# The sample's differential keys and values: fetched page by page by SyncE through a register, in place of GpSimd's row gathers

## The chip, the cores and the metric

One program on one core of a Trainium2 chip computes a whole decoder layer. The metric is the device time of the program in microseconds, the median of several executions. The core has five engines that run their own instruction streams and meet only at semaphores: TensorE (PE, its weight loads are shown as PEld), VectorE (DVE), ScalarE (ACT), GpSimd (POOL) and SyncE (SP). All of them can issue transfers, which run on the core's 16 DMA engines.

## The reference, cut to what matters

The layer runs for a prompt of 1024 tokens and for a sample group of 8 sequences with 4 new tokens each. Each sample sequence has 4096 past tokens in a paged cache. A page holds 128 tokens, and `page_table` (8 x 32, int32) says which page of the pool holds which part of a sequence. The part that the change touches is the sample's differential attention:

```
def gather_pages(pool, page_table):
    rows = pool[page_table]
    return rows.reshape((page_table.shape[0], -1) + pool.shape[2:])
...
def diff_sample(qb, kb, vb, cache_k, cache_v, page_table, bias_b, lam, lam_init, subln_g):
    t = qb.shape[1]
    past = page_table.shape[1] * cache_k.shape[1]
    k_all = jnp.concatenate([gather_pages(cache_k, page_table).astype(kb.dtype), kb], axis=1)
    v_all = jnp.concatenate([gather_pages(cache_v, page_table).astype(vb.dtype), vb], axis=1)
    return diff_core(qb, k_all, v_all, past + jnp.arange(t), jnp.arange(past + t), bias_b, lam, lam_init, subln_g)
```

All of `cache_b_k` and `cache_b_v` that the table names is read: 8 sequences x 32 pages x 128 tokens x 512 float32, for keys and again for values, 134 MB in all. The same sample group also has a selective attention ("A", smaller caches `cache_a_k`, `cache_a_v`) and an indexer (`cache_idx_k`), which the change leaves with GpSimd.

## The kernel before

The program is a row of stages. The one that matters is `selective_and_sample_stage`. In it two streams of steps are interleaved into one fixed order (function `beside`), the same on PE, ACT and DVE: the prompt's selective attention (lines 1374 to 1500) and the sample's attention (class `Walk` and `sample_attention`). GpSimd and SyncE have their own programs in the stage, `pool` and `sync`.

The sample's attention first scores the indexer's keys (steps "i"), then walks over chunks of past tokens. There are 32 differential ("B") chunks, 16 for each of two groups g of four sequences, then the selective ("A") ones. A B chunk is 256 tokens, that is two pages, of four sequences j = 0 to 3. Its data are a **unit** u: four tiles of keys and four of values, each 128 partitions x 1024 float32 (512 KB), 4.19 MB together. Partition p of a tile holds two neighbouring tokens (`RKB` is 2), so a page of 128 tokens fills 64 partitions, and the chunk's first page lies in partitions 0 to 63, the second in 64 to 127.

On PE, a chunk n goes through these steps: "k" transposes the keys of each j through PSUM (line 1875, two banks of four transposes each; ACT copies each bank out, line 2004), "s" makes the logits (line 1895), DVE takes their maximum (line 2130), ACT the exponential (line 2014), "p" transposes the probabilities (line 1937), and "o" multiplies them with the values (line 1958). The keys of chunk n + 1 are turned before the outputs of chunk n. Steps "c" (lines 1852 and 2058) are a search for the indexer's threshold, and lines 1412 to 1438 belong to the prompt's stream; both fill the time between.

Keys have one buffer for each j (`kv[:, j, :]`, in the tile `region`), so the keys of unit u + 1 may be fetched once PE has turned those of u (semaphore `t_full`). Values have two: `kv[:, 4 + j, :]` for even units, and for odd ones `apart` (tiles `sa_more_values` and `side`); those of unit u may be fetched once unit u - 2 has been used (`pv_done`). GpSimd fetches both: `gather_rows` (line 1109) is one indirect DMA of 128 rows of 4 KB, whose row numbers stand in a column of the table `gather_b`, computed once by DVE. It issues the four keys of a unit as their buffers come free, and then the four values. SyncE has little to do in the stage: one load at its start, half of `w_out` when the mask is ready (line 1788), and the other half after the last output.

Of the kernel before, what the change touches and what calls it, by code (L numbers as in the profile page):

```python
# [22 lines left out]
P = 128  # L23
# [190 lines left out]
class Setup:  # L214
# [57 lines left out]
    def other_loads(self, sp):  # L272
        M, io = self.M, self.io

        def load(dst, src):
            sp.dma_start(dst, src).then_inc(self.loaded, 16)
            self.n_loaded += 16
        load(M.const[:], io["consts"][:, 0:M.const.shape[1]])
        load(M.const_setup, io["consts"][:, M.const.shape[1]:])
        load(self.rb32, io["rel_bias"][:])  # L280
        for t in range(4):
            load(self.rb4[32 * t:32 * t + 32, :], io["rel_bias"][:])
        load(M.gain_ak[:], io["a_k_norm"][0].partition_broadcast(P))
# [71 lines left out]
    def dve(self, eng, s, room):  # L355
# [38 lines left out]
        if 2 <= s < 5:  # L394
            n, rk, table = (("b", RKB, M.gather_b), ("a", RKA, M.gather_a), ("i", RKI, M.gather_i))[s - 2]
# [1162 lines left out]
class Walk:  # L1558
# [73 lines left out]
    def keys_arrivals(self, u, j):  # L1632

        if u < self.first_a:
            return NCI + u + 1
        i = self.turn(u, j)
        return (NCI + self.first_a if i % 6 < 4 else self.first_a // 2) + i // 6 + 1

    def values_arrivals(self, u, j):

        if u < self.first_a:
            return (u + 1) // 2 if self.aside(u) else NCI + u // 2 + 1
        i = self.turn(u, j)
        return (NCI if i % 6 < 4 else 0) + self.first_a // 2 + i // 6 + 1
# [14 lines left out]
def sample_attention(nc, io, M, K, S):  # L1659
# [7 lines left out]
    kv_rows = {("B", 0): io["cache_b_k"][0].rearrange("n (s r) h c d -> (n s) (r h c d)", r=RKB),  # L1667
               ("B", 1): io["cache_b_v"][0].rearrange("n (s r) h d -> (n s) (r h d)", r=RKB),
               ("A", 0): io["cache_a_k"][0].rearrange("n (s r) g d -> (n s) (r g d)", r=RKA),
# [26 lines left out]

    def keys_at(u, j):

        x = walk.turn(u, j) % 6 if u >= walk.first_a else j
        return (kv[:, x, :], loaded[x]) if x < 4 else (apart[x - 4], M.gathered_apart[x - 4])  # L1700

    def values_at(u, j):

        if walk.aside(u):
            return apart[j], M.gathered_apart[j]
# [9 lines left out]
    def pool(eng):  # L1715
# [17 lines left out]
        def keys(u, js=range(4)):  # L1733
            for j in js:
                i = walk.turn(u, j)
                if u == 0:
                    eng.wait_ge(t_full, fill["i", NCI - 1, 0, 1, j] + 1)
                elif i < 4:
# [7 lines left out]
        def values(u):  # L1746
            for j in range(4):
                i = walk.turn(u, j)
                if u == 0:
                    eng.wait_ge(t_full, fill["i", NCI - 1, 1, 1, j] + 1)  # L1750
                elif u == 1 and j == 0:
                    eng.wait_ge(sc_mm, NCI)
                elif 0 <= i - 4 < 2:
# [11 lines left out]
        keys(0)  # L1765
        values(0)
        for u in range(1, len(walk.units)):
# [1516 lines left out]
def build(nc, io, const_at):  # L3284
    with ExitStack() as ctx:
# [7 lines left out]
        M.x_loaded = [ctx.enter_context(nc.semaphore(f"x_loaded{t}")) for t in range(NT)]  # L3293
        M.gathered_apart = [ctx.enter_context(nc.semaphore(f"gathered_apart{i}")) for i in range(4)]
# [34 lines left out]
        with ExitStack() as c1:  # L3329
# [10 lines left out]
            with ExitStack() as c2:  # L3340
                M.bias_s = sb(c2, "bias_s", [P, 2, P])
                M.bias_new = sb(c2, "bias_new", [P, 2, 2, NS])
                M.gather_b = sb(c2, "gather_b", [P, DEC_B * NCB], I32)
# [134 lines left out]
```

## Time and profile before

| | |
|---|---|
| median of 3 runs | 2584.93 us (2583.08 to 2594.52) |
| the profiled execution | span 2590.7 us |
| PE busy | 2312.3 us, 89% of the span |
| DVE, ACT, POOL busy | 1103.6, 766.2 and 660.5 us (43%, 30%, 25%) |
| moved by GpSimd's queue (q0) | 48384 packets, 176.18 MB |
| moved by SyncE's queue (q1) | 80774 packets, 90.50 MB |

The span runs from the first to the last instruction of one execution, taken by the profiler; that execution lies 5.8 us above the median. Busy time is summed over the whole program, though the stages have different limits, so the stage that the change touches (about 565 us to 1330 us) has to be read by itself. Issuing a DMA does not count as busy time on SP; an indirect DMA on POOL does.

### The profile page before, as it was taken

The numbers are of one execution on the slowest core, as the hardware profiler recorded it, in microseconds if no ns is written. First come the engines' busy times: TensorE is split into PE (matmuls) and PEld (weight loads), VectorE is DVE, ScalarE is ACT, GpSimd is POOL, SyncE is SP. The second block draws the span as 40 slices with busy tenths as digits, with TensorE's granted clock in tenths as the row PEclk, the third lists the DMA queues.
The fourth block names the chain that finished last, engine by engine and source line by source line (L and its number), as shares of the span: only waits on it lengthen the run. The fifth ranks groups of instructions, "written<-read, shape, count | busy, mean of one in ns | idle before, by whom it ended". The sixth has DMA issues, their size and how long they took to land. (4 is left out here: it accounts for less than half of the span.)

```text
span 2590.7 us, 32530 instructions
## 1 busy us (share of the span) xinstructions
PE 2312.3 (89%) x12169; PEld 1549.6 (60%) x12189; DVE 1103.6 (43%) x2687; ACT 766.2 (30%) x2065; POOL 660.5 (25%) x703
## 2 busy tenths in 40 slices
PE   7999997767777878788789898899999999999999
PEld 5644443443455455555444445548888888888887
DVE  5489998742445533333322212352443343371001
ACT  3551345653444444444421013311111111110000
POOL 1451223123544445433301010013222121201110
PEclk9999998988889889998889999999999999999999
DMA  4211101025888778765540014111111111122221
GB/s 140 73 60 70 38 9 65 1 82 188 275 277 269 234 266 281 257 213 193 173 162 28 33 49 163 34 67 34 50 34 50 34 50 40 44 65 74 74 63 39
DMA packets 147603, 281.75 MB, mean 109 GB/s; under 512 B 13479, under 2 KB 82775, under 8 KB 147447
## 3 DMA queue, kind: packets, MB, share of 16 engines
q0 software_dynamic: 48384, 176.18, 20.2%
q1 hardware_dynamic: 80774, 90.50, 10.6%
q10 hardware_dynamic: 18288, 12.98, 1.7%
q8 instruction: 99, 1.62, 0.2%
q14 instruction: 58, 0.47, 0.1%
HBM read 261.68 MB, written 17.94 MB: 108 GB/s over the span
## 5 line engine op out<-in xcount | busy, mean ns | idle before, releaser
L634 PE MATMUL PS<-region 128*128 128x512 f32 (+5 forms) x864 | 327.7, 534 | 1.8 <-DMA region<-w_in 1.8
L2784 PE MATMUL PS<-region,ffn_w 128*128 128x264 f32 x1408 | 323.1, 388 | 1.6 <-PEq L2234 1.6
L2784 PEld LDWEIGHTS PS<-region,ffn_w 128*128 128x128 f32 x1408 | 269.2, 191 | 48.4 <-issue 1.9
L2004 ACT COPY region<-PS 128x512 f32<-128x512 f32 x352 | 197.2, 591 | 212.6 <-PE PS L1868 72.2
L634 PEld LDWEIGHTS PS<-region 128*128 128x128 f32 (+1 forms) x864 | 152.7, 181 | 161.2 <-issue 140.9
L2784 PE MATMUL PS<-region,side 128*128 128x264 f32 x1056 | 245.0, 389 | 1.8 <-POOL side L2741 1.8
L1875 PE MATMUL PS<-ident_f,region 128*128 128x128 f32 x1024 | 170.7, 316 | 82.4 <-ACT region L2004 44.1
L2784 PEld LDWEIGHTS PS<-region,side 128*128 128x128 f32 x1056 | 200.0, 191 | 35.8 <-POOL side L2741 1.9
L1875 PEld LDWEIGHTS PS<-ident_f,region 128*128 128x128 f32 x1024 | 133.5, 162 | 117.0 <-issue 76.3
L931 DVE TENSOR_SCALAR_CACHE_REDUCE mask<-score,cand 128x384 bf16<-128x384 f32 (+2 forms) x198 | 180.9, 942 | 3.4
L1109 POOL DMA_INDIRECT region<-cache_b_k,gather_b x128 | 120.4, 941 | 212.0 <-PE PS L1875 177.8
L2739 POOL TENSOR_TENSOR side<-ffn_w 128x512 f32<-128x512 f32 x22 | 28.4, 1290 | 393.2 <-DMA ffn_w<-w_gate 199.6
L2931 DVE TENSOR_TENSOR ffn_gb<-PS,ffn_u 128x264 f32<-128x264 f32 (+2 forms) x66 | 20.5, 338 | 183.2 <-ACT ffn_u L2895 120.7
L2304 PE MATMUL PS<-side,QTB 128*128 128x512 f32 x192 | 85.4, 594 | 0.9 <-PEq L2660 0.9
L2374 DVE TENSOR_TENSOR region<-PS,region 128x512 f32<-128x512 f32 (+1 forms) x36 | 24.8, 688 | 136.3 <-PE PS L2304 136.3
L2150 DVE SCALAR_TENSOR_TENSOR sa_oacc<-sa_oacc,sa_alpha,PS 128x512 f32<-128x512 f32 (+1 forms) x48 | 29.5, 614 | 100.2 <-PE PS L1958 82.3
L1109 POOL DMA_INDIRECT region<-cache_b_v,gather_b x64 | 60.2, 940 | 42.1 <-PE PS L1958 20.7
L3120 PE MATMUL PS<-H,ffn_w 128*128 128x264 f32 x308 | 69.8, 386 | 1.3 <-PEq L2728 1.3
L2130 DVE TENSOR_REDUCE sa_cmax<-PS 128x1 f32<-128x256 f32 (+2 forms) x48 | 23.1, 482 | 110.6 <-remote 86.2
L2864 ACT COPY side<-PS 128x264 f32<-128x264 f32 x44 | 16.7, 379 | 180.6 <-PE PS L2784 180.6
L1478 DVE TENSOR_REDUCE sa_a_far_max<-PS 128x1 f32<-128x16 f32 (+6 forms) x56 | 31.8, 569 | 88.7 <-PE PS L1419 71.1
L3258 DVE TENSOR_TENSOR dn_rest<-PS,dn_rest 128x512 f32<-128x512 f32 (+2 forms) x24 | 11.6, 510 | 135.4 <-PE PS L3131 134.9
(448 smaller groups left out, 4017.7 us busy)
## 6 DMA issues: line engine op xcount, KB each, us to landing
ffn_w<-w_gate SPq DMA_DIRECT2D x11, 1024.0 KB, 5.4
ffn_w<-w_up SPq DMA_DIRECT2D x11, 1024.0 KB, 5.5
region<-w_in SPq DMA_DIRECT2D x4, 2048.0 KB, 7.9
ffn_w<-w_down ACTq DMA_DIRECT2D x7, 704.0 KB, 5.6
region<-x_prompt ACTq DMA_DIRECT2D x8, 512.0 KB, 7.1
region<-x_prompt SPq DMA_DIRECT2D x8, 512.0 KB, 10.6
mem_keys<-cache_mem_k SPq DMA_DIRECT2D x8, 512.0 KB, 5.0
mem_values<-cache_mem_v SPq DMA_DIRECT2D x8, 512.0 KB, 8.0
```

What stands on the lines that cost most here:

```text
L634: last = nc.tensor.matmul(M.PS[0:n, s % 3, 0:chunks[j].width], XT[:, c, t * P:t * P + n], w[j % 2][:, c, 0:chunks[j].width], start=(c == 0 ...
L931: self.link.send(nc.vector.tensor_scalar(self.mask[:, sc], self.score[:, sc], as_float[:, x:x + 1], 0.0, op, ALU.add, accum_out=self.count ...
L1109: nc.gpsimd.indirect_dma_start(out, None, src, bass.IndirectOffsetOnAxis(ap=table[:, col:col + 1], axis=0)).then_inc(arrived, 16)
L1478: nc.vector.tensor_reduce(far_max[:, e:e + 1], slot(e, 0, lo), axis=AX.X, op=ALU.max).then_inc(far_done, 1)
L1875: last = nc.tensor.transpose(t[:, q * P:(q + 1) * P], keys[:, r * 512 + m * P:r * 512 + (m + 1) * P], K("ident"))
L2004: nc.scalar.copy(dst, M.PS[0:dst.shape[0], T0 + x % 2, 0:dst.shape[1]]).then_inc(t_read, 1)
L2150: nc.vector.scalar_tensor_tensor(oacc[:, 0:kw], oacc[:, 0:kw], alpha[:, x], M.PS[:, L1, 0:kw], ALU.mult, ALU.add).then_inc(o_done, 1)
L2304: last = nc.tensor.matmul(M.PS[:, s % 4, :], lhs(c, t), w[q][:, c, :], start=(c == 0), stop=(c == kc - 1))
L2374: nc.vector.tensor_tensor(x, M.PS[0:n, s % 4, :], x, ALU.add).then_inc(added, 1)
L2739: nc.gpsimd.tensor_tensor(ws[:, 0], a21, a22, ALU.add).then_inc(made, 1)
L2784: last = nc.tensor.matmul(M.PS[:, bank, 0:TW], left[:, c, :], right[:, c, :], start=begin and c == 0, stop=(c == KH - 1), skip_group_check ...
L3120: last = nc.tensor.matmul(M.PS[:, bank + x, 0:TW], left[:, c, :], right[:, c, x * TW:(x + 1) * TW], start=begin and c == 0, stop=(c == KH ...
```

## The change

SyncE takes over the 256 fetches of the B units. It loads the page table itself into an 8 x 32 tile, `pages`. For each unit, each j and each of its two pages it reads the page number into a register (`value_load`), and issues a plain DMA from that page into the 64 partitions that belong to it. The eight registers read for a unit's keys are used again for its values. So a tile comes in two DMAs of 256 KB where it came in one gather of 512 KB: 512 DMAs and 256 register loads in place of 256 gathers. The waits are the same ones, in the same order, now on SyncE. The B tiles get semaphores of their own, since the counts of the gathers' semaphores now hold only indexer and A fetches; the table `gather_b` and the four DVE instructions that made it go.

```diff
@@ other_loads
+        sp.dma_start(M.pages[:], io["page_table"][:]).then_inc(M.pages_loaded, 16)
...
@@ pool
-            if kind == "B":
-                gather(out, arrived, kv_rows[kind, v], M.gather_b, (4 * g + j) * NCB + c)
-            else:
-                gather(out, arrived, kv_rows[kind, v], M.gather_a, (4 * g + j) * NCA + c // HALVES)
+            gather(out, arrived, kv_rows[kind, v], M.gather_a, (4 * g + j) * NCA + c // HALVES)
...
-        keys(0)
-        values(0)
-        for u in range(1, len(walk.units)):
+        for u in range(walk.first_a, len(walk.units)):
...
@@ sync
+        half, n_pool = P // 2, io["cache_b_k"].shape[1]
+        eng.wait_ge(M.pages_loaded, 16)
+        for u in range(walk.first_a):
+            kind, g, c = chunks[walk.units[u]]
+            page = {}
+            for v in range(2):
+                for j in range(4):
+                    b = 4 * g + j
+                    if v == 0 and u == 0:
+                        eng.wait_ge(t_full, fill["i", NCI - 1, 0, 1, j] + 1)
+                    elif v == 0:
+                        eng.wait_ge(t_full, fill["k", walk.units[u - 1], j, 1] + 1)
+                    elif u == 0:
+                        eng.wait_ge(t_full, fill["i", NCI - 1, 1, 1, j] + 1)
+                    elif u == 1 and j == 0:
+                        eng.wait_ge(sc_mm, NCI)
+                    elif j == 0:
+                        eng.wait_ge(pv_done, walk.units[u - 2] + 1)
+                    out, arrived = (values_at if v else keys_at)(u, j)
+                    for i in range(2):
+                        if v == 0:
+                            page[j, i] = eng.value_load(M.pages[b:b + 1, 2 * c + i:2 * c + i + 1], min_val=0,
+                                                        max_val=n_pool - 1)
+                        eng.dma_start(out[half * i:half * (i + 1), :],
+                                      pages_b[v][bass.ds(page[j, i], 1)].rearrange("o s f -> (o s) f")
+                                      ).then_inc(arrived, 16)
         for x in range(2):
             if x == 0:
                 eng.wait_ge(mask_ready, 1)
```

GpSimd's program in the stage before, from the indexer's gathers to the B values of unit 3 (`gather_i`, `gather_b` are the tables of row numbers; brackets name the semaphores waited for):

```order
L1109 DMA region<-cache_idx_k,gather_i 128x1024 [waits sa_t_full] x4
L1109 DMA region<-cache_b_k,gather_b 128x1024 [waits sa_t_full] x4
L1109 DMA region<-cache_b_v,gather_b 128x1024 [waits sa_t_full] x4
L1109 DMA region<-cache_b_k,gather_b 128x1024 [waits sa_t_full] x4
L1109 DMA sa_more_values<-cache_b_v,gather_b 128x1024 [waits sa_sc_mm]
L1109 DMA sa_more_values<-cache_b_v,gather_b 128x1024
L1109 DMA side<-cache_b_v,gather_b 128x1024 x2
L1109 DMA region<-cache_b_k,gather_b 128x1024 [waits sa_t_full] x4
L1109 DMA region<-cache_b_v,gather_b 128x1024 [waits sa_pv_done]
L1109 DMA region<-cache_b_v,gather_b 128x1024 x3
```

The same place of GpSimd's program after the change:

```order
L1110 DMA region<-cache_idx_k,gather_i 128x1024 [waits sa_t_full] x4
L1110 DMA region<-cache_a_k,gather_a 128x1024 [waits sa_t_full] x4
L1110 DMA region<-cache_a_v,gather_a 128x1024 [waits sa_pv_done]
L1110 DMA region<-cache_a_v,gather_a 128x1024 x3
L1110 DMA sa_more_values<-cache_a_k,gather_a 128x1024 [waits sa_pv_done] x2
```

All 256 B gathers are gone from GpSimd, and the A gathers follow the indexer's at once. SyncE's program in the stage before, whole (it ends with the first loads of the next stage):

```order
L1536 UNCONDITIONAL_BRANCH [waits barrier_Pool_Activation_PE_DVE_SP_release]
L1399 DMA bias_a<-bias_scratch 128x8x256
L1788 DMA side<-w_out 128x4x512 [waits sa_mask_ready]
L1788 DMA side<-w_out 128x4x512 [waits sa_pv_done]
L1535 UNCONDITIONAL_BRANCH
```

SyncE's program after it, from the last two keys of unit 0 to the first key of unit 1 (`TENSOR_LOAD` is the register load; each `ISA` row is a register operation or check that belongs to it or to the DMA's address):

```order
L1799 TENSOR_LOAD pages [waits sa_t_full]
L1799 ISA x2
L1801 ISA
L1801 DMA region<-cache_b_k 64x1024
L1799 TENSOR_LOAD pages
L1799 ISA x2
L1801 ISA
L1801 DMA region<-cache_b_k 64x1024
L1801 DMA region<-cache_b_v 64x1024 [waits sa_t_full]
L1801 DMA region<-cache_b_v 64x1024
L1801 DMA region<-cache_b_v 64x1024 [waits sa_t_full]
```

Each key half is four rows, of which the first, the register load, stands behind the wait; each value half is one. The two `w_out` loads now stand behind all of them.

## Rows read from the trace of the kernel before

**Rows 1.** The page: span, DMA share and rate in 40 slices of 64.8 us.

```profile
span 2590.7 us, 32530 instructions
DMA  4211101025888778765540014111111111122221
GB/s 140 73 60 70 38 9 65 1 82 188 275 277 269 234 266 281 257 213 193 173 162 28 33 49 163 34 67 34 50 34 50 34 50 40 44 65 74 74 63 39
```

**Rows 2.** Windows: the stretch from unit 1's first key to unit 31's, and two pieces.

```profile
core 0: us, PE busy (x) PEld busy (x) DVE busy (x) ACT busy (x) POOL busy (x), PEclk, DMA share, GB/s
650.00:700.00 50.00, 37.45 (x298) 24.21 (x298) 21.25 (x76) 20.90 (x62) 24.30 (x26) 0.86 0.83 277
...
1050.00:1100.00 50.00, 38.84 (x356) 25.70 (x350) 15.93 (x44) 21.31 (x50) 24.36 (x27) 0.93 0.80 265
626.00:1102.00 476.00, 374.99 (x3200) 242.98 (x3212) 197.08 (x600) 210.02 (x538) 227.80 (x240) 0.90 0.80 266
```

**Rows 3.** Timeline of POOL: first key gathers of units 1 and 31, and unit 6.

```profile
626.49 0.94 POOL L1109 DMA_INDIRECT region<-cache_b_k,gather_b  x1 [13.92 <-PE PS L1875]
...
700.85 0.94 POOL L1109 DMA_INDIRECT region<-cache_b_k,gather_b  x1 [2.75 <-PE PS L1875]
...
706.40 0.94 POOL L1109 DMA_INDIRECT region<-cache_b_k,gather_b  x1 [0.95 <-PE PS L1875]
708.28 0.94 POOL L1109 DMA_INDIRECT region<-cache_b_v,gather_b  x1 [0.94 <-PE PS L1958]
...
712.01 0.94 POOL L1109 DMA_INDIRECT region<-cache_b_v,gather_b  x1 [0.30 <-issue]
...
715.46 0.94 POOL L1109 DMA_INDIRECT region<-cache_b_k,gather_b  x1 [2.51 <-PE PS L1875]
...
1102.28 0.93 POOL L1109 DMA_INDIRECT region<-cache_b_k,gather_b  x1 [1.36 <-remote]
```

**Rows 4.** Timeline of all engines, 707 to 716 us: one unit's logits and what follows.

```profile
708.22 1.93 PE L1895 MATMUL PS<-region,QBB 128*32 128x256 f32 x32
711.17 0.63 PE L1875 MATMUL PS<-ident_f,region 128*128 128x128 f32 x4
714.00 0.42 DVE L2130 TENSOR_REDUCE sa_cmax<-PS 128x1 f32<-128x256 f32 x1 [3.13 <-remote]
714.04 0.37 ACT L1447 COPY region<-PS 128x256 f32<-128x256 f32 x1 [5.56 <-remote]
714.53 0.66 PE L1875 MATMUL PS<-ident_f,region 128*128 128x128 f32 x4 [2.73 <-ACT sa_total L2004]
```

**Rows 5.** Waits: us in total, times, longest; then SyncE's own.

```profile
DVE sa_cmax L2130 <- remote: 80.4, 25, 5.3
...
SPq L1788 <- PE PS L1958: 430.2, 1, 430.2
SPq L1788 <- DVE sa_mask L2071: 332.4, 1, 332.4
```

**Rows 6.** Page, DMA issues: KB each, median us to landing. Stores of full and of 32 partitions.

```profile
x_scratch<-region SPq DMA_DIRECT2D x8, 512.0 KB, 2.6
p_b_v<-in_nat SPq DMA_DIRECT2D x8, 256.0 KB, 2.0
p_idx_k<-in_nat SPq DMA_DIRECT2D x8, 32.0 KB, 1.4
x_scratch<-region SPq DMA_DIRECT2D x1, 128.0 KB, 1.9
s_b_k<-in_kd SPq DMA_DIRECT2D x1, 64.0 KB, 1.6
s_idx_k<-in_nat SPq DMA_DIRECT2D x1, 8.0 KB, 1.4
```

**Rows 7.** DMA view of 1338 to 1365 us, 40 slices: SyncE's loads of 128 partitions.

```profile
GB/s 12 0 115 231 346 413 401 325 407 394 397 361 407 410 416 437 416 407 437 419 407 437 419 401 437 407 328 194 285 373 413 407 407 413 407 443 422 407 376 61
```

**Rows 8.** Timeline of SP: issues of plain loads, one behind the other.

```profile
1340.62 3.58 SPq L202 DMA_DIRECT2D region<-x_prompt  x6
...
1582.46 1.93 SPq L2550 DMA_DIRECT2D mem_keys<-cache_mem_k  x4
```

More of the change, by code:

```diff
@@ L393, in dve @@
             link(nc.vector.tensor_scalar(M.gain_sub[:], M.gain_sub[:], 1.0 - LAM0, None, ALU.mult))
-        if 2 <= s < 5:
-            n, rk, table = (("b", RKB, M.gather_b), ("a", RKA, M.gather_a), ("i", RKI, M.gather_i))[s - 2]
+        if 3 <= s < 5:
+            n, rk, table = (("a", RKA, M.gather_a), ("i", RKI, M.gather_i))[s - 3]
             pages = self.pt_f.rearrange("p (u i) -> p u i", i=rk)
@@ L1634, in keys_arrivals @@
         if u < self.first_a:
-            return NCI + u + 1
+            return 2 * (u + 1)
         i = self.turn(u, j)
-        return (NCI + self.first_a if i % 6 < 4 else self.first_a // 2) + i // 6 + 1
+        return (NCI if i % 6 < 4 else 0) + i // 6 + 1
     def values_arrivals(self, u, j):
         if u < self.first_a:
-            return (u + 1) // 2 if self.aside(u) else NCI + u // 2 + 1
+            return 2 * (u // 2 + 1)
         i = self.turn(u, j)
-        return (NCI if i % 6 < 4 else 0) + self.first_a // 2 + i // 6 + 1
+        return (NCI if i % 6 < 4 else 0) + i // 6 + 1
     def rescaled(self, n):
@@ L1666, in sample_attention @@
     idx_rows = index_rows(io)
-    kv_rows = {("B", 0): io["cache_b_k"][0].rearrange("n (s r) h c d -> (n s) (r h c d)", r=RKB),
-               ("B", 1): io["cache_b_v"][0].rearrange("n (s r) h d -> (n s) (r h d)", r=RKB),
-               ("A", 0): io["cache_a_k"][0].rearrange("n (s r) g d -> (n s) (r g d)", r=RKA),
+    pages_b = (io["cache_b_k"][0].rearrange("n (s r) h c d -> n s (r h c d)", r=RKB),
+               io["cache_b_v"][0].rearrange("n (s r) h d -> n s (r h d)", r=RKB))
+    kv_rows = {("A", 0): io["cache_a_k"][0].rearrange("n (s r) g d -> (n s) (r g d)", r=RKA),
                ("A", 1): io["cache_a_v"][0].rearrange("n (s r) g d -> (n s) (r g d)", r=RKA)}
@@ L1695, in sample_attention @@
     loaded = M.gathered
+    keys_loaded, values_loaded, apart_loaded = ([S.sem(f"{n}_loaded{j}") for j in range(4)]
+                                                for n in ("keys", "values", "apart"))
     def keys_at(u, j):
+        if u < walk.first_a:
+            return kv[:, j, :], keys_loaded[j]
         x = walk.turn(u, j) % 6 if u >= walk.first_a else j
@@ L1702, in values_at @@
     def values_at(u, j):
-        if walk.aside(u):
-            return apart[j], M.gathered_apart[j]
+        if u < walk.first_a:
+            return (apart[j], apart_loaded[j]) if walk.aside(u) else (kv[:, 4 + j, :], values_loaded[j])
         x = walk.turn(u, j) % 6 if u >= walk.first_a else j
@@ L1735, in keys @@
                 i = walk.turn(u, j)
-                if u == 0:
-                    eng.wait_ge(t_full, fill["i", NCI - 1, 0, 1, j] + 1)
-                elif i < 4:
+                if i < 4:
                     turned(u - 1, j)
@@ L1748, in values @@
                 i = walk.turn(u, j)
[L1749 to L1753, printed above, removed]
+                if 0 <= i - 4 < 2:
                     used(walk.first_a - 1)
@@ L3293, in build @@
         M.x_loaded = [ctx.enter_context(nc.semaphore(f"x_loaded{t}")) for t in range(NT)]
+        M.pages_loaded = ctx.enter_context(nc.semaphore("pages_loaded"))
         M.gathered_apart = [ctx.enter_context(nc.semaphore(f"gathered_apart{i}")) for i in range(4)]
@@ L3342, in build @@
                 M.bias_new = sb(c2, "bias_new", [P, 2, 2, NS])
-                M.gather_b = sb(c2, "gather_b", [P, DEC_B * NCB], I32)
+                M.pages = sb(c2, "pages", [DEC_B, PAST // PAGE], I32)
                 M.gather_a = sb(c2, "gather_a", [P, DEC_B * NCA], I32)
```

## The prediction

> **What bounds the kernel now.** I began with the page's slices: over the whole span the DMA engines are little used, but from 650 us on there is a plateau, shares of 7 to 8 tenths and 234 to 281 GB/s, which lasts until about 1100 us [rows 1]. That is the walk over the B units, the only place that the change touches. The timeline of POOL gives its pace: unit 1's first key gather starts at 626.49 us and unit 31's at 1102.28 [rows 3]. So 30 units take 476 us, 15.9 us each. In that stretch PE is busy 375.0 of 476 us (79%, 12.5 us for each unit), POOL 227.8, DVE 197.1, ACT 210.0; the DMA engines are at 0.80 with 266 GB/s [rows 2]. 266 GB/s x 15.9 us is 4.2 MB, one unit. So no engine is full; PE and the DMA engines are nearest, both at 80%, and 3.4 us of each unit are lost on PE.
>
> Where they are lost shows in one unit. PE issues its logits at 708.22 for 1.93 us, four key transposes at 711.17, and then nothing until 714.53 [rows 4]. DVE, which waits for those logits, starts at 714.00, and ACT, which waits for a transpose of the prompt's stream, at 714.04, both with a releaser that the profile can't name ("remote"). So what PE had finished by 710.2 reached the others 3.8 us later, all at once. In the same time POOL issues its four value gathers, the last at 712.01 for 0.94 [rows 3], and the release comes 1.05 us after its end. The waits of DVE for the logits with this unnamed releaser sum to 80.4 us in 25 times [rows 5], which is 3.2 us each and most of PE's loss. I read it as a side effect of back-to-back gathers on GpSimd, though one trace doesn't prove it. Whatever its cause, it is what this change could give back.
>
> **The change, part by part.**
>
> *POOL* loses 256 gathers of 0.94 us. They are not its bound (227.8 of 476 us), so nothing comes from its time as such. If the late releases of PE come from the gathers, up to 3.2 us for each unit is free: 30 x 3.2 = 96 us.
>
> *SyncE's issues.* SyncE waits idle for 332.4 and 430.2 us in this stage [rows 5], so its time is free, but its pace counts. It must issue 16 DMAs and 8 register loads in each unit. A plain load is issued in 0.48 us (1.93 for 4) to 0.60 us (3.58 for 6) [rows 8]; I take 0.48, since these are smaller, and 16 make 7.7 us. A register load is nowhere in the trace. From below it costs nothing; from above I take the smallest transfer's whole way, 1.4 us from issue to landing of 8 KB [rows 6], since a load of one word can hardly take longer, with its register operations. So SyncE needs 7.7 to 7.7 + 8 x 1.4 = 18.9 us for each unit. I keep both ends. As to the waits: the register load stands behind the wait for `t_full`, and what is queued behind it on SyncE is the rest of the unit and, at the very end, half of `w_out`, which is needed only in the next stage: it was issued at once when the mask was ready and will now go out some 300 us later, still before the A chunks end. A key's way gets longer by a register load, but a key buffer is refilled most of a period before PE wants it (released and gathered at 700.85, next turned at 711.17), so up to some us more are hidden.
>
> The Trainium skill gives a floor for such a load (DMA: Bandwidth & Descriptors, section "Latency and other measured facts"): about 600 ns. With it SyncE would need 12.5 us for a unit, and would bound nothing.
>
> *The transfers.* This is the term on which the sign rests. The bytes are the same, but each DMA now covers 64 partitions, and 16 engines serve it. Loads of 128 partitions on SyncE's queue run at a plateau of 407 GB/s, the value that comes most often in [rows 7]. Stores show what a narrow tile does. With all 128 partitions 32, 256 and 512 KB land after 1.4, 2.0 and 2.6 us [rows 6]: 1.37 us fixed, and 480 KB more in 1.2 us, about 410 GB/s. A tile of 32 partitions with 128 KB takes 1.9 us. On the full tiles' line it would be 1.37 + 0.32 = 1.69; it takes 0.53 us behind the fixed part, that is 247 GB/s (64 KB in 1.6 agree with 285). With landings rounded to 0.1 us, the 128 KB allow 207 to 291. So a tile in a part of the partitions moves at half to seven tenths of the full rate.
>
> A unit at 247 GB/s takes 4.19 / 0.247 = 17.0 us, at half of the loads' plateau (204 GB/s) 20.6 us, and at the full 407 only 10.3. I take 20.6. Half is what would come out if the write side of half the partitions has half the width, and the DMAs alternate between the halves in one queue, so that all 16 engines are in the same half at the same time. The store rows are single transfers whose fixed part hides some of their slowness, so I lean to the low rate.
>
> What SBUF — State Buffer in the Trainium skill says of this (section "Door 1: The DMA port swizzle") speaks against the change outright: partitions 0 to 63 reach only 8 of the 16 ports, measured there at 196 GB/s for 1 MiB against 328 for all 128. Its next section but one ("Can I just issue two DMAs to hit both halves?") adds that two concurrent DMAs on the two halves gain only 6% over one. At 196 GB/s a unit would take 21.4 us and the sum below would be 2751. The store rows agree in direction, and with a smaller loss.
>
> *Start and small things.* Unit 0 is fetched in the pause before 626 us, which has 14 us to spare [rows 3]. The four DVE instructions and the page table's load lie in the first stage beside other work. The A units are gathered as before.
>
> **Sum.** The walk becomes bound by the transfers: 30 x 20.6 = 618 us for 476, so +142. SyncE (at most 18.9 us) and PE (12.5 us) fit below that. What the gathers' end gives back to PE vanishes in the new wait, for keys and values in flight. The prompt's steps are spread through the same walk and wait with it. 2590.7 + 142 = 2733 for the profiled execution; the median lies 5.8 us below it, which gives **2727 us**.
>
> **The rivals.**
>
> 1. *The halves run together and PE is the bound (faster).* If the 16 engines drift apart, some in the lower half and some in the upper, or a narrow load is simply as fast as a wide one, transfers need 10.3 us. If then a register load costs less than (12.5 - 7.7) / 8 = 0.6 us, PE's 12.5 us rule: 30 x (12.5 - 15.9) = -101 us, 2484. For it: the late releases of PE would be gone with the gathers. Against it: the store rows, and two unknowns have to come out well at once. It turns slower where a unit needs more than 15.9 us, that is below 264 GB/s or above 1.0 us for a register load.
> 2. *Full rate, but SyncE paces.* With 1.0 us for a register load nothing changes; at 1.4 us a unit takes 18.9, +91 us, 2676.
> 3. *Narrow rate as in the stores, 17.0 us:* +33, 2618.
> 4. *SyncE is slower than I bound it.* With 2.0 us for a load and its register operations it needs 23.7 us: +235, 2820. Then keys would be what PE waits for, and SyncE would never be idle.
>
> **How the numbers follow.** Chances: the forecast 0.52, rival 1 0.20, rival 2 0.10 (half of it within 0.5% of no change), rival 3 0.08, rival 4 0.10. So faster 0.20, same 0.05, slower 0.75; 0.5% is 13 us and about what a measurement of this kernel can tell from no change. The forecast's own range is 2680 to 2770: 19.0 us for a unit, and 22.0 where waits couple with a full queue. For 8 in 10 the range has to reach to both sides: up to rival 4, 2830, and down to 2500, where rival 1 has come out all but wholly; what is left out is rival 1's best case and a worse rival 4.
>
> **What would show it.** In the profile after, the first and the last B key load should lie about 618 us apart, the windows between at some 205 GB/s with a high DMA share, as packets of 4 KB take twice as long. PE's busy time in that stretch stays at 375 us but falls to 60% of it, and its waits stand before the key transposes or the outputs. DVE's unnamed waits for the logits should be gone or rare if the gathers cause them; if they stay, that reading was wrong. SyncE should show issues of about 0.5 us and pauses in front of `t_full`; if it has none, rival 4 or 2 holds. The forecast is wrong if the rate in that stretch is above 264 GB/s.

## The result, and the profile after

The changed kernel takes 2616.1 us (median of 4, 2603.1 to 2624.2), the kernel before on the same chip 2587.4 (4 runs): a ratio of 1.011, 95% interval 1.0076 to 1.0145. It is slower, by 29 us (1.1%) and not by the 140 forecast; the range held the time. The profiled execution has a span of 2614.4 us, 23.7 more than before.

The page of the kernel after, the same lines as in [rows 1]:

```profile
span 2614.4 us, 34354 instructions
PEclk9999997988778888989879999999999999999999
DMA  3211101026999899995532023211111111122221
GB/s 138 73 59 70 38 9 65 1 86 177 243 251 251 238 230 248 279 273 192 179 124 104 2 79 123 71 67 34 33 50 49 34 50 34 49 65 69 74 63 42
```

The plateau of the B walk is still there, but most of its DMA shares are 9 tenths where they were 7 and 8, and it moves a little less: full engines, fewer bytes. The windows over the walk, to be laid beside [rows 2] (the third is again unit 1's first key to unit 31's):

```profile
650.00:700.00 50.00, 36.96 (x260) 24.90 (x264) 17.73 (x61) 20.08 (x54) 0.00 (x0) 0.76 1.04 242
1050.00:1100.00 50.00, 43.23 (x370) 28.34 (x370) 16.37 (x45) 23.39 (x56) 0.00 (x0) 0.90 1.03 283
627.66:1132.42 504.76, 396.79 (x3215) 257.79 (x3215) 196.72 (x600) 215.13 (x544) 0.00 (x0) 0.85 1.01 248
```

POOL is empty, the DMA share is 1.01 and the rate 248 GB/s. A unit takes 504.76 / 30 = 16.8 us in place of 15.9. That is +29 us. What comes before unit 1 takes 1 us more than before and what follows unit 31's first key 6 us less (2614.4 - 1132.4 against 2590.7 - 1102.3), so the walk is the whole difference. SyncE's timeline, which takes the place of POOL's in [rows 3]:

```profile
627.66 9.57 SPq L1801 DMA_DIRECT2D region<-cache_b_k  x8
637.33 2.45 SPq L1801 DMA_DIRECT2D sa_more_values<-cache_b_v  x4
639.88 2.46 SPq L1801 DMA_DIRECT2D side<-cache_b_v  x4
...
1132.42 9.54 SPq L1801 DMA_DIRECT2D region<-cache_b_k  x8
```

Eight keys with their register loads take 9.6 us, eight values 4.9: 14.5 us of a 16.8 us unit. The timeline of all engines around one unit's logits, which answers to [rows 4], and the page's DMA issues (KB each, median us from issue to landing):

```profile
716.62 1.93 PE L1916 MATMUL PS<-region,QBB 128*32 128x256 f32 x32
...
718.96 0.37 ACT L1448 COPY region<-PS 128x256 f32<-128x256 f32 x1 [2.07 <-PE PS L1428]
...
719.15 0.42 DVE L2151 TENSOR_REDUCE sa_cmax<-PS 128x1 f32<-128x256 f32 x1
```

```profile
region<-cache_b_k SPq DMA_DIRECT2D x256, 256.0 KB, 11.0
region<-cache_b_v SPq DMA_DIRECT2D x128, 256.0 KB, 10.8
```

The logits end at 718.55 and DVE reads them at 719.15, with no wait of its own in between; before it waited 3.13 us, with no releaser named. But a 256 KB key now needs 11 us to land, since it stands in a full queue. The waits of 600 to 1148 us (us in total, times, longest):

```profile
PEld PS L1896 <- DMA region<-cache_b_k: 100.1, 58, 5.1
PE PS L1896 <- DMA region<-cache_b_k: 80.0, 45, 4.8
DVE sa_cmax L2151 <- PE PS L1916: 17.9, 14, 2.7
...
SPq L1799 <- PE PS L1896: 51.0, 40, 11.1
```

DVE's 80.4 us of unnamed waits for the logits [rows 5] are gone. In their place TensorE waits 80.0 us for keys in flight.

### The profile page after: what moved, and what is told of

Its sections match the earlier page's. It is cut to its first block and busy times, and to the rows that moved or that the text cites. A ratio compares the mean times of both kernels' runs of the same rounds, so it can differ in the third digit from the quotient of the medians.

```text
span 2614.4 us, 34354 instructions
## 1 busy us (share of the span) xinstructions
PE 2335.7 (89%) x12189; PEld 1564.2 (60%) x12189; DVE 1102.1 (42%) x2683; ACT 769.3 (29%) x2065; POOL 418.1 (16%) x447
## 5 line engine op out<-in xcount | busy, mean ns | idle before, releaser
L1896 PE MATMUL PS<-ident_f,region 128*128 128x128 f32 x1024 | 180.2, 331 | 93.2 <-DMA region<-cache_b_k 80.0
L1896 PEld LDWEIGHTS PS<-ident_f,region 128*128 128x128 f32 x1024 | 144.3, 171 | 127.7 <-DMA region<-cache_b_k 100.1
L1110 POOL DMA_INDIRECT region<-cache_a_k,gather_a x22 | 21.4, 972 | 583.7 <-PE PS L1896 558.9
L1240 ACT ACTIVATE region<-PS,pb_negmax 128x384 f32<-128x384 f32 (+5 forms) x96 | 54.6, 578 | 49.8 <-DVE pb_negmax L1334 33.3
L1188 PE MATMUL PS<-KTB,QTB 64*128 64x384 f32 (+5 forms) x192 | 50.8, 621 | 20.1 <-ACT region L1240 16.6
```

The costliest lines, as they stand in the source:

```text
L1188: last = nc.tensor.matmul(out[:, k], M.QTB[s, h, i * P:(i + 1) * P], M.KTB[s, h, a:b], start=True, stop=True)
L1240: nc.scalar.activation(prob[:, 2 * (n % 2) + k, a:b], slot(piece0[n] + x, b - a)[:, k], ACT.Exp, bias=negmax[:, n % 2, k:k + 1], accum_out ...
L1896: last = nc.tensor.transpose(t[:, q * P:(q + 1) * P], keys[:, r * 512 + m * P:r * 512 + (m + 1) * P], K("ident"))
```

## The experiments

Each was timed against the kernel before on the same chip, but they ran on different chips (e1 to e4 on one; e5 to e8, e9 to e12, e13 to e15 each on one of their own; the changed kernel apart from them). A difference of two medians from different chips is therefore given by the ratios too, as a share of 2587 us. Ratios have their 95% interval. "Fixed pages" marks kernels whose B tiles come from page numbers set at build time in place of the page table's. A unit's time is from the first and the last unit on SyncE's timeline.

| kernel | median us | ratio to before |
|---|---|---|
| changed kernel | 2616.1 | 1.011 (1.0076 to 1.0145) |
| e1 halves, fixed pages | 2593.7 | 1.0026 (0.9992 to 1.0060) |
| e2 128 partitions, fixed pages | 2482.5 | 0.9599 (0.9572 to 0.9626) |
| e3 page over 128 partitions | 2513.1 | 0.9710 (0.9683 to 0.9738) |
| e4 values grouped by half | 2644.3 | 1.0229 (1.0196 to 1.0261) |
| e5 e2 + 4 small gathers a unit | 2584.4 | 0.9946 (0.9925 to 0.9966) |
| e6 e3 with fixed pages | 2487.7 | 0.9579 (0.9556 to 0.9601) |
| e7 e3, register loads first | 2516.8 | 0.9694 (0.9675 to 0.9713) |
| e8 changed kernel, loads first | 2614.2 | 1.0065 (1.0040 to 1.0090) |
| e9 e5 with 16 rows | 2586.1 | 0.9995 (0.9982 to 1.0008) |
| e10 e5 with one gather | 2488.0 | 0.9616 (0.9600 to 0.9632) |
| e11 e2 + GpSimd arithmetic | 2483.1 | 0.9601 (0.9585 to 0.9617) |
| e12 e3, values by GpSimd | 2490.9 | 0.9628 (0.9612 to 0.9645) |
| e13 lower halves only | 2493.9 | 0.9665 (0.9649 to 0.9681) |
| e14 e1, halves paired | 2633.3 | 1.0215 (1.0185 to 1.0246) |
| e15 a queue for each half | 2536.9 | 0.9836 (0.9817 to 0.9856) |

### Is it the width of the transfer? (e1, e2)

e1 takes away the register loads and keeps the two DMAs of 64 partitions:

```diff
-                        if v == 0:
-                            page[j, i] = eng.value_load(...)
+                        at = (b * NCB * 2 + 2 * c + i) % n_pool
                         eng.dma_start(out[half * i:half * (i + 1), :],
-                                      pages_b[v][bass.ds(page[j, i], 1)]...
+                                      pages_b[v][at:at + 1]...
```

> The changed kernel with fixed page numbers: the same 512 DMAs of 64 partitions on SyncE, but no register load (each B tile gets pages by count, not by the page table). Theory W (a tile in 64 partitions is written at a reduced rate, 249 GB/s in the walk after the change): nothing moves, since only SyncE's pace changes; 2616 us within 10, 16.8 us for a unit, 4 KB packets at 0.27 us. Rival I (SyncE's issuing paces the walk: 9.2 us for eight keys and 5.0 for eight values, 14.3 of 16.8 us): without the loads SyncE needs 16 x 0.62 = 9.9 us for a unit, and the walk falls towards PE's 12.5 to 14 us, 2490 to 2535 us.

e2 takes two neighbouring pages in one DMA of 128 partitions:

```diff
+                    at = (b * NCB * 2 + 2 * c) % n_pool
+                    eng.dma_start(out, pages_b[v][at:at + 2]...).then_inc(arrived, 16)
```

> As e1_half_static, but the two pages of a tile are neighbours in the pool and come in one DMA of 128 partitions x 4 KB (256 DMAs of 512 KB; page numbers fixed, not by the page table). Theory W: packets fall back to 0.16 us, the transfers need 10.3 us for a unit, and PE's 12.5 to 13.5 us become the bound: 2485 to 2520 us, below the kernel before, because GpSimd's gathers and the late releases beside them are gone too. A rival by which HBM or SyncE's queue as such is slow at these loads: the same as e1_half_static, at or above 2600 us. If the late releases had nothing to do with the gathers, they are seen again and the time is 2570 to 2590, that of the kernel before.

e1 came out at 2593.7, e2 at 2482.5: the same bytes, packets of the same 4 KB, 111 us apart. The windows 650 to 700 us, of e1 and then of e2 (columns as in [rows 2]):

```profile
650.00:700.00 50.00, 34.67 (x282) 22.08 (x282) 19.27 (x64) 19.22 (x55) 0.00 (x0) 0.88 1.04 239
```

```profile
650.00:700.00 50.00, 44.66 (x436) 27.80 (x424) 32.15 (x110) 28.31 (x83) 0.00 (x0) 1.00 1.00 380
```

Both have full DMA engines here; the wide tiles move 380 GB/s, the narrow ones 239, and PE issues 436 matmuls in place of 282. In e2 a unit takes 12.6 us (622.5 to 1001.8 us for 30), in e1 15.9 in a profiled execution that lies 12 us below its median. The 12.6 look like PE's 12.5 us of before, but are made up otherwise: PE is busy for 339.25 us of e2's walk, 11.3 a unit, and idle for 1.3. So the narrow tile is what bounds the changed kernel. e2 came out just under what theory W gave it; e1 missed both of its expectations, 22 us below theory W's 2616 and far above rival I, so what the register loads cost is not nothing. e1 against the changed kernel prices them at about 22 us, at the medians and by the ratios, but e1's runs lie wide, from 2570 to 2619 (without the two longest its median is 2590.7), and the two intervals of the ratio all but touch. e1 also reads other pages of the pool, which no run here keeps apart from the loads, and the DMA share is full with them and without (1.01 and 1.03 over the walk), so how they cost time is open.

### How fast is a half? (e4, e13, e14, e15)

e4 issues a unit's values as four lower halves and then four upper ones:

```diff
+            for i in range(2):
+                for j in range(4):
+                    out, arrived = values_at(u, j)
+                    eng.dma_start(out[half * i:half * (i + 1), :], pages_b[1][bass.ds(page[j, i], 1)]...
```

> The changed kernel, but the eight value DMAs of a unit go out as four to partitions 0 to 63 and then four to 64 to 127, in place of alternating; the rest is the same. If the 249 GB/s (above half of the full plateau of 407) come from engines that have drifted into different halves, the values now move at 204 GB/s: 2.1 MB take 10.3 in place of 8.4 us, +1.9 us for a unit, +57 us, 2665 to 2680 us. If the rate of a half doesn't depend on what the others do: 2616 us within 10.

It took 28 us more than the changed kernel (31 by the ratios), about half of the 57 that drifted engines were to cost and clearly more than the rival's nothing. e14 changes only the order in e1, so that neighbours in the queue share a half:

```diff
-                    for i in range(2):
+                    for i in ((0, 1), (1, 0))[j % 2]:
```

> The kernel with fixed page numbers and 64-partition DMAs (2594 at the median), with the halves of every second tile issued in the other order: lower, upper, upper, lower, so that two neighbours in the queue are in one half. Theory M: the queue's engines work a DMA or two apart, and it is this spread over the halves that lifts the rate above half. Then it falls a little, as with the grouped values: 2600 to 2640. Rival: the order of the halves doesn't matter: 2570 to 2619, as without.

It took 2633.3, 40 us more than e1 (49 by the ratios), with the same instructions and bytes. The walks of the two, unit 1's first key to unit 31's, e1 and then e14, both at a full DMA share:

```profile
623.60:1100.97 477.37, 378.58 (x3219) 243.84 (x3219) 196.11 (x601) 213.78 (x545) 0.00 (x0) 0.90 1.03 261
625.11:1134.28 509.17, 383.39 (x3093) 249.44 (x3093) 191.52 (x585) 207.60 (x524) 0.00 (x0) 0.85 1.03 236
```

e13 fetches, from unit 2 on, the lower halves alone, and leaves old data in the upper ones:

```diff
-                    for i in range(2):
+                    for i in range(2 if u < 2 else 1):
```

> The kernel with fixed page numbers and 64-partition DMAs, but from unit 2 on only the lower half of each tile is fetched (the upper half keeps old data), so half the bytes. Theory H: one half alone moves at half the full rate. Packets of 4 KB then take 0.32 us (twice 0.159), the rate while they move is 204 GB/s, a unit needs 2.1 MB / 204 = 10.3 us, and TensorE's 12.5 us bind: 2482 to 2500. Rival: a half alone is already as fast as the mixture of the changed kernel: packets of 0.26 us, the same time.

Its time, 2493.9, says only that TensorE is the bound again. What it was made for is the rate. The DMA view of 650 to 700 us, 40 slices of 1.25 us, first of e13, then of e2, then of the changed kernel:

```profile
DMA  9999999999999999899999957599988846389999
GB/s 206 206 210 203 203 200 206 206 213 200 197 206 206 210 210 203 161 243 200 206 210 203 206 121 200 108 288 206 197 190 213 128 154 203 66 256 206 210 210 200
```

```profile
GB/s 413 393 413 419 416 413 413 413 413 406 410 406 410 413 410 410 403 383 364 390 387 416 367 374 397 341 282 295 311 262 324 351 406 383 413 380 377 292 334 383
```

```profile
GB/s 239 239 249 226 252 256 226 252 236 239 256 239 239 252 226 243 243 243 246 256 229 252 252 229 249 246 229 249 236 246 246 249 233 233 239 249 226 256 236 239
```

One half alone moves 206 GB/s with all engines full, half of the 413 of the wide tiles. Halves that alternate in one queue move 226 to 256 in this window, 242 on the mean; paired (e14) the same window has 221, at a full share too. So a half is at half the rate, as forecast, and what the forecast missed is that alternating halves do better. That the order alone moves the rate is measured; that the engines are then in different halves at one time is the reading of it, since no view shows which half an engine is writing. e15 mixes them on purpose, lower halves by SyncE and upper by GpSimd, both with the page number in a register:

```diff
+        # GpSimd: the same loop, with i = 1
-                    for i in range(2):
+                    for i in (0,):
```

> The changed kernel with all lower halves by SyncE and all upper halves by GpSimd (plain DMAs with the page number in a register of GpSimd, which in the kernel with values by GpSimd delayed nobody). Theory M: with a queue for each half both halves are in flight together all the time, the rate goes up to 330 to 400 GB/s, and TensorE's 12.6 us bind: 2485 to 2510. Rival: the engines take the two queues in turn and a packet into half the partitions stays slow: 2580 to 2620.

2536.9 us, 79 less than the changed kernel (71 by the ratios) and between the two expectations. Its window:

```profile
650.00:700.00 50.00, 40.92 (x337) 26.73 (x339) 20.92 (x72) 25.64 (x71) 13.93 (x27) 0.89 1.03 294
```

294 GB/s at a full share, and 291 over its walk (626.68 to 1053.31 us): the mixture is better, but not full. SBUF — State Buffer in the Trainium skill (section "Can I just issue two DMAs to hit both halves?") says that two concurrent DMAs on the two halves gain 6% over one. Here 294 against e13's 206 is 43% more, and even one queue of alternating halves gains 17% (242 in the window of the changed kernel); the measurement decides. The same page's figure for one half, 196 GB/s for 1 MiB (section "Door 1: The DMA port swizzle"), is near the 206.

### SyncE's pace (e3, e6, e7, e8)

e3 keeps the page table, the register loads and 16 DMAs a unit, but spreads each page of 128 tokens over 128 partitions, 2 KB each. The order of the tokens within a tile changes, so one bias moves with it:

```diff
-                      out[half * i:half * (i + 1), :]
+                      out[:, 512 * i:512 * (i + 1)]
...
-                    for r in range(RKB):
-                        ... M.PS[:, L0, r * P + 64:(r + 1) * P], K("ident"), M.bias_s[:, 1, r:P:RKB]
+                        ... M.PS[:, L0, P:2 * P], K("ident"), M.bias_s[:, 1, 0:P]
```

> The changed kernel with another layout of the B tiles: a page's 128 tokens lie in 128 partitions, 2 KB each, the second page in the second half of the columns; register loads, number and size of the DMAs as in the changed kernel, and the whole computation is done. Theory W: width is restored, packets of 2 KB take 0.08 to 0.09 us, and SyncE's 14.3 us for a unit become the bound: 14.4 to 15.5 us, 2545 to 2580 us, faster than before. Rival I: SyncE's work is unchanged, so 2600 to 2616 us stay. A third outcome, that many small packets cost as much as narrow tiles: 2616 or more.

2513.1 us: 103 less than the changed kernel with the same work for SyncE, and 2.9% less than before. That is 32 us below the best that was expected, since SyncE, with a less full queue, needs 12.3 us for a unit in place of 14.5 (rows below). A unit takes 13.7 us, 1.1 above e2's. e6 takes the loads out of e3:

> The kernel with a page over 128 partitions, its page numbers fixed (the B pages are not those of the page table) and no register loads; still two DMAs of 2 KB a partition for each tile. Theory S: at 13.7 us for a unit that kernel goes at SyncE's pace (8 loads and 16 issues), so without the loads it reaches the PE-bound 12.6 us of the 128-partition kernel: 2482 to 2490. Rival: the second DMA and its 2 KB packets are what costs the 31 us. Then it stays at 2505 to 2515.

2487.7: theory S holds, the loads cost 25 us (34 by the ratios), and two DMAs of 2 KB a partition cost next to nothing (e2 has 2482.5). e6 reads other pages of the pool too, but e12 below, which reads the table's, lies only 3 us above it (13 by the ratios). Unit 0's keys on SyncE's timeline, with a nearly empty queue, of e3 and of e6:

```profile
600.92 8.35 SPq L1801 DMA_DIRECT2D region<-cache_b_k  x8
609.38 3.91 SPq L1801 DMA_DIRECT2D region<-cache_b_v  x8
```

```profile
601.12 3.67 SPq L1798 DMA_DIRECT2D region<-cache_b_k  x8
```

A plain issue takes 3.67 / 8 = 0.46 us, an issue whose address comes from a loaded register 3.91 / 8 = 0.49, and a register load with its range check (8.35 - 3.91) / 8 = 0.56 us, or 0.58 with the dearer issue behind it. The Trainium skill gives about 600 ns as the floor of such a load (DMA: Bandwidth & Descriptors, section "Latency and other measured facts"); this trace agrees for the load with its check, while the load instruction alone takes 0.27 us in the changed kernel.

e7 moves the eight loads of a unit in front of its first wait, in e3:

```diff
+            page = {(j, i): eng.value_load(...) for j in range(4) for i in range(2)}
             for v in range(2):
...
-                        if v == 0:
-                            page[j, i] = eng.value_load(...)
```

> The same kernel with a page over 128 partitions and all its page numbers from the table, but the eight register loads of a unit stand before its first wait, where SyncE would otherwise be idle. Theory S: the loads, about 0.5 us each, no longer lie between a buffer coming free and its DMA. 2485 to 2500. Rival: SyncE is occupied for nearly the whole 13.7 us of a unit, so where the loads stand makes no difference: 2508 to 2516.

Nothing came of it (2516.8): the rival holds, SyncE is occupied for 12.3 (8.35 + 3.91) of 13.7 us, and it is the amount of its work that counts. e8 is the same edit in the changed kernel:

> The changed kernel (64-partition DMAs) with its eight register loads of a unit moved before the unit's first wait. Theory W: the transfers bound the walk, SyncE needs 14.3 of the 16.8 us of a unit, so this gives nothing to 22 us (what leaving the loads out altogether gave): 2594 to 2616. Rival: the loads between the issues are a real part of the walk's loss against before; then it falls to before's 2584 or below.

2614.2, within both kernels' scatter (2 us less, 12 by the ratios, whose intervals overlap). Where the transfers bound, the place of the loads is worth nothing that these runs can tell either.

### What delayed TensorE's releases before? (e5, e9 to e12)

e5 puts gathers back beside e2, small ones, in the place of the value gathers of before:

```diff
+        for u in range(2, walk.first_a):
+            used(u - 2)
+            for j in range(4):
+                ...
+                gather(small[:, j, :], small_loaded[j], small_rows, M.gather_a, j * NCA)
```

> The kernel with one 128-partition DMA per tile and fixed page numbers, and beside it on GpSimd 28 times four small gathers (128 rows of 64 bytes each into a buffer that nobody reads), issued where the value gathers of the kernel before stood. Theory G: what delays the release of TensorE's waiters in the kernel before (VectorE waited 80.4 us with no releaser named for the logits of the walk) is GpSimd's gather itself. Then these waits come back, 50 to 90 us of them, and the time goes from 2482 to 2520 to 2570. Rival: the delay came from the 512 KB that a gather moves, or from transfers that filled the DMA engines. Then the small gathers cost nothing, 2480 to 2492, and the waits without a releaser stay at a few us.

2584.4: 102 us more than e2 at the medians (by the ratios, 0.9946 - 0.9599, 90 us), above what either theory allowed, for 120 gathers of 8 KB whose data nobody reads (the units are 30, not the 28 of the expectation). One unit in e5's timeline, all engines:

```profile
748.69 0.94 POOL L1110 DMA_INDIRECT sa_small<-cache_idx_k,gather_a  x1 [10.89 <-PE PS L1985]
...
749.91 1.93 PE L1922 MATMUL PS<-region,QBB 128*32 128x256 f32 x32
749.94 0.94 POOL L1110 DMA_INDIRECT sa_small<-cache_idx_k,gather_a  x1 [0.31 <-issue]
...
752.44 0.94 POOL L1110 DMA_INDIRECT sa_small<-cache_idx_k,gather_a  x1 [0.30 <-issue]
...
754.53 0.42 DVE L2157 TENSOR_REDUCE sa_cmax<-PS 128x1 f32<-128x256 f32 x1 [1.69 <-remote]
754.57 0.16 ACT L2031 COPY sa_total<-PS 128x1 f32<-128x1 f32 x1 [5.68 <-remote]
```

It is [rows 4] again; of the four gathers, the third is left out. The logits end at 751.84, and DVE and ACT are let go together at 754.5, 1.15 us after the end of the last gather (753.38). It is no accident of one unit: in the 27 groups of four gathers in e5's walk whose rows the timeline shows one by one, the first waiter starts 0.99 to 1.21 us after the end of the last gather. DVE's waits for the logits in the walks of e5, e10 and e11:

```profile
DVE sa_cmax L2157 <- remote: 77.8, 24, 5.3
```

```profile
DVE sa_cmax L2157 <- remote: 4.7, 1, 4.7
```

```profile
DVE sa_cmax L2157 <- remote: 4.6, 1, 4.6
```

Why it is more than the 77.8 us of waits shows in the windows over the two walks, e2's and then e5's:

```profile
622.48:1001.75 379.27, 339.25 (x3211) 214.39 (x3211) 195.41 (x598) 206.44 (x537) 0.00 (x0) 0.98 0.90 329
626.82:1099.94 473.12, 379.11 (x3198) 245.18 (x3211) 196.88 (x598) 209.49 (x537) 106.94 (x113) 0.89 0.79 266
```

Of e5's 94 us more, PE is idle for 54 and busy for 40 longer with the same matmuls, as its mean granted clock falls from 0.98 to 0.89. This mean is made of two levels, 1.00 (2.4 GHz) and 0.50 (1.2 GHz): in e5 PE is busy for 0.07 us between 706 and 708 us, and the clock stands at 0.50 from 708 to 712; in e2 it is 1.00 from 700 to 760. So a late release costs its pause and, behind it, slower matmuls.

The three that follow say what it is about the gathers. e9 gives them 16 rows in place of 128:

```diff
-                gather(small[:, j, :], small_loaded[j], small_rows, M.gather_a, j * NCA)
+                gather(small[0:16, j, :], small_loaded[j], small_rows, M.gather_a[0:16], j * NCA)
```

> The kernel of the small gathers (fixed page numbers, 128-partition DMAs, 28 times four gathers on GpSimd that nobody reads), with 16 rows a gather in place of 128. Theory G1: what holds up TensorE's releases is in proportion to the rows, each of which is a descriptor that GpSimd writes. Then an eighth of the 102 us stays: 2490 to 2505, and GpSimd's gather gets shorter than 0.94 us. Rival G2: it is each gather instruction, whatever its rows. Then it stays at 2565 to 2590.

2586.1, no less: it is the instruction, not its rows (a gather took 0.84 us on the mean in place of 0.95). e10 leaves one of the four (`for j in range(1)`):

> The same with 128 rows, but one gather a unit in place of four. If every gather costs alike (102 us for 112 of them, 0.9 us each): 28 of them make 2482 + 26 = 2508. If a unit pays once, for the group, whatever its length: up to 2550. If the gathers' cost lies only in their run of four, which outlasts TensorE's slack: 2485 to 2495.

2488.0: one gather a unit costs next to nothing (4 to 6 us more than e2, within the scatter of the ratios), and the waits are those of e2. A lone gather holds back no release: beside the one of 875.04 to 875.98 us, ACT starts on TensorE's results at 875.36 and DVE at 875.90. e11 has four small powers on GpSimd in their place:

```diff
-                gather(small[:, j, :], ...)
+                nc.gpsimd.tensor_tensor(small[:, j, 8:12], small[:, j, 0:4], M.neg_half[:, 0:4], ALU.pow)
```

> The kernel with one 128-partition DMA per tile and fixed page numbers, and on GpSimd, where the small gathers stood, 28 times four small powers (128 x 4 elements, about 1 us each) in place of gathers. Theory G: arithmetic on GpSimd holds nobody's release up, 2480 to 2490. Rival: any work of GpSimd at that place does it (a port or the core shared with it), 2530 to 2590.

2483.1: arithmetic of the same length (3.93 us for the four) holds up nobody. e12, last, is e3 with the values fetched by GpSimd, as plain DMAs with the page number in its register:

```diff
+        # GpSimd
+        for u in range(walk.first_a):
+            ...
+                    page = eng.value_load(M.pages[b:b + 1, 2 * c + i:2 * c + i + 1], ...)
+                    eng.dma_start(out[:, 512 * i:512 * (i + 1)], pages_b[1][bass.ds(page, 1)]...
```

> The kernel with a page over 128 partitions (from the page table), keys by SyncE and values by GpSimd: plain DMAs with the page number in a register of GpSimd. SyncE then has 8.5 us of work in a unit in place of 13.4. Theory S: the walk goes at TensorE's pace and the time falls from 2513 to 2485 to 2495. Rival: GpSimd writes the descriptors of its plain DMAs itself, as in a gather, and TensorE's releases come late beside them: 2540 to 2640.

2490.9 us, 3.7% less than before (interval 0.9612 to 0.9645): the best kernel here that reads the page table. GpSimd's timeline in e12:

```profile
747.00 0.55 POOL L1777 DMA_DIRECT2D sa_more_values<-cache_b_v  x1 [5.05 <-issue]
748.15 0.55 POOL L1777 DMA_DIRECT2D sa_more_values<-cache_b_v  x1 [0.60 <-issue]
749.29 0.55 POOL L1777 DMA_DIRECT2D sa_more_values<-cache_b_v  x1 [0.60 <-issue]
```

Eight of these in a row, 0.55 us each and 0.60 apart for the register load, and TensorE's waiters are not held up (DVE's unnamed waits for the logits are 5.8 us, once). Whether the kind of the instruction or the wider gap spares them was not tried.

## Why the prediction was right and wrong

The +29 us come apart with the runs. Without the gathers, and with tiles as wide as before, the kernel takes 102 us less than before on the same chip (2584.4 to 2482.5, e2), of which e5 gives 90 to 102 to the late releases. The 64-partition tiles take 111 back (e2 to e1), and the register loads, with the weaker evidence said above, 22. These three steps add up to the whole change by construction (-102 + 111 + 22 = +31; measured +29 on its own chip), so the sum tests nothing; each step stands on its own pair of runs.

- **What bounds the kernel before: right in the cause, lucky in the size.** The late releases beside the gathers, read from one trace, are shown by e5, e9, e10 and e11. The 96 us that they were said to be worth are 90 to 102. But the 96 were 30 waits of 3.2 us with PE's busy time left as it is, and in e5 only 54 us are idle time of PE; 40 are its slower clock, which the forecast did not have.
- **The step that failed** is in *The transfers*: "the DMAs alternate between the halves in one queue, so that all 16 engines are in the same half at the same time". Half the width is half the rate for a half alone (e13: 206 GB/s against 413). But alternating halves move 248 GB/s over the walk and not 204, so the term is 16.8 us a unit in place of 20.6, and 30 x 3.8 = 114 us too much were summed. That is all of the miss of 113 us (+142 forecast, +29 measured). That the order of the halves makes the rate is shown by e14 and e4 (28 to 49 us slower); e15, with a queue for each half, is 71 to 79 us faster, though it also halves SyncE's work, which e1 and e8 price at 2 to 22 us here.
- **A smaller term was put at nothing:** "SyncE (at most 18.9 us) and PE (12.5 us) fit below that". The 16.8 us hold about 22 us of register loads in 30 units; without them (e1) a unit takes 15.9 us, so the transfers' own term was too high by 4.7.
- **Rival 3, with 0.08, is what happened** (17.0 us a unit forecast, 16.8 measured; 2618 and 2616). Its number came from a store of 32 partitions, and neither the mixing nor the register loads were in it. The fixed part of 1.37 us behind it is also a little high: a line through the three full stores has 1.33, which makes the narrow store 230 GB/s, a unit 18.2 us and the time 2655. So that it hits so well is luck, in the main. Still the nearest row gave the better rate; the forecast left it for a mechanism that no row showed.
- **SyncE: the bounds held.** 7.7 us of issues were right on an empty queue (16 x 0.46 to 0.49), and the load with its register operations costs 0.56 to 0.58 us, inside 0 to 1.4. On the full queue an issue takes 0.61 us (4.91 for 8), and a unit takes SyncE 14.5 us. Rivals 2 and 4 are out. In e3, where the transfers are fast, SyncE's pace is the next bound, worth 25 to 34 us.
- **Rival 1** failed on the rate: e2 reaches its 2484 with wide tiles (2482.5), and e12, which reads the page table, nearly (2490.9). That the number fits is luck again: it took PE's 12.5 us as the floor, and e2's 12.6 are 11.3 busy at a clock of 0.98 and 1.3 idle.
- **What the profile was to show.** The walk was to last 618 us and lasted 504.8; the windows were to have 205 GB/s and had 248, still below the 264 that would have turned the sign. Packets were to take twice as long; the share over the rate went from 0.80 / 266 to 1.01 / 248, 1.35 times. DVE's unnamed waits are gone, TensorE waits in front of the key transposes, and SyncE pauses for `t_full` (51.0 us in 40 times), all as said. PE's busy time was to stay at 375 us and fall to 60% of the stretch; it is 396.8 us for the same 3,200 matmuls, 79% of the stretch. The granted clock of the stretch fell from 0.90 to 0.85, and 375 x 0.90 / 0.85 = 397.

## What to carry to other kernels

Lay a paged tile out so that every DMA spans all 128 partitions, be it with shorter rows (2 KB here): that was worth 103 us of 2616. Where a row of the trace and a mechanism in your head give two rates, the row is the forecast and the mechanism the rival. Before moving gathers off GpSimd for its own sake, look for waits on TensorE whose releaser has no name beside them: here GpSimd was never the bound, and that side effect of its gathers was all there was to win. Count what a pause on TensorE costs with the clock behind it, not the pause alone.

## What the runs showed of the hardware

- Gathers back to back on GpSimd (0.30 us apart) hold up the waiters of TensorE until 0.99 to 1.21 us after the last one ends (27 groups of e5; 1.05 in the unit shown of the kernel before); four of them in each of 30 units cost 90 to 102 us, with 128 or with 16 rows. One alone held back no release (e10, the one of 875.04 us) and cost nothing that shows, nor did arithmetic or plain DMAs with a register load between them. By which path the release is held is open.
- Behind such a pause TensorE's granted clock falls from 1.00 to 0.50 for some us; in e5 that is 40 of the 94 us by which its walk is longer than e2's.
- One half of the partitions is written at 206 GB/s, all of them at 413. Over the walk, halves in one queue give 261 alternating (e1), 248 alternating with register loads between the issues (the changed kernel), 236 paired (e14), and a queue each 291 (e15). Why two queues don't reach more was not tried.
- A load of a page number into a register of SyncE with its range check costs 0.56 to 0.58 us, an issue 0.46 to 0.49 us on an empty queue and 0.61 in the full one of 64-partition tiles.
